# Stages that end with four weight pieces used by token tile, the next stage's first tile turned among them, and rings of seven and five places

## The chip, the cores and the metric

The kernel runs on one core of one Trainium2 chip. The metric is the device time of one execution in microseconds (us); the median of three runs was 2169.57 us (2169.47 to 2170.34).

## The reference, cut to what matters

Two blocks of two layers each work on 256 tokens of 1024 features, in float32. A layer of the first block is

```
x = x + 0.5 * rmsnorm(swiglu(rmsnorm(x, g1), gate, up, down), p1)     # hidden width 2816
x = x +       rmsnorm(token_mixing(rmsnorm(x, g2)) @ w_out, p2)       # chunk band, differential, stick-breaking heads
x = x + 0.5 * rmsnorm(swiglu(rmsnorm(x, g3), gate, up, down), p3)
```

and a layer of the second block is

```
merged = sum over 3 branches of sigmoid gate * (branch output @ w_branch)   # sparse, gated linear, memory attention
x = x + merged @ w_out
x = x + relu(rms_norm(x, g) @ w_up)**2 @ w_down                             # hidden width 4096
```

What matters here: ten stages follow one another (three for each layer of the first block, two for each of the second). Each begins with features of x (a root mean square norm whose scale is applied when the first products are taken out of PSUM) and ends with an output product that is added to x, in the first block after a norm of its own, in the second block plainly.

## The kernel before, in words

**Pieces.** All weights come as one stream of 616 pieces of 128 x 1024 floats, in the order in which TensorE uses them. A float32 product is made of three TensorE products: each piece is split into a rounded high part `hi` and the rest `lo`, as are the activations, and `product` (L513) issues high by high, high by low, low by high. A piece is twelve such products of 512 columns: six for each of the two token tiles (128 tokens each).

**The way of a piece.** SP's program (`piece`, L409) issues its DMA into `raw`; ACT (`round_piece`, L1131) writes the rounded `hi`; POOL (`pool_program`, L484) writes `lo = raw - hi`; TensorE uses it and counts it in the semaphore `used`. Each of the three rings has RING = 4 places (L30). The DMA of piece c waits for `lo` of piece c - 4, the rounding for the landing and for `used` of piece c - 4, POOL for `hi`. ACT's program places the rounding of a piece AHEAD = 3 pieces (L31) ahead of its use, between its other work. `in_mixer` (L476) says which pieces POOL subtracts in four parts of 256 columns; the others are one instruction.

**A stage's start.** `enter_stage` (L598) calls `enter` (L574): TensorE turns token tile 0 of x (`turned_tile`, L559: eight 128 x 128 transposes into four PSUM banks, a pair to a bank), ACT copies each out as `h_hi`, DVE makes `h_lo`. Then TensorE uses the first four pieces for tile 0, turning tile 1 after the second and third, and then the same four pieces for tile 1. Only then are these four counted as used. ACT's `features` (L1162) takes the squares of x for the norm between.

**A stage's end.** `last_rows` (L547) uses the last pieces of the output product (two in the first block, in the second mixer's last branch and its output product; four in the second block's feed-forward) for tile 0, signals `f`, and then for tile 1. ACT (`last_rows`, L1198) takes the squares of the output of tile 0 at `f` (`row_squares`, L1184), the guess of the root (`row_guess`, L1191), then those of tile 1; DVE multiplies by the gain (`row_gain`, L1618) and adds to x in two halves (`row_add`, L1626), each of which counts in the semaphore `x` that the turn waits for. In the second block DVE only adds (`add_plain`, L1644).

**Orders.** Each engine runs its program in order. The mixers' orders are written out by `mix1_order` (L62) and `mix2_order` (L135): attention units stand between strips (four pieces of an input product) and rows (one piece of an output product). Parameter loads stand in SP's program, one after every three pieces.

## Time and profile before

| | |
|---|---|
| profiled execution | 2170.57 us, span 2169.0 us |
| median of the runs | 2169.57 us |
| TensorE busy | 2079.8 us, 96% |
| ScalarE (ACT), VectorE (DVE), GpSimd (POOL) busy | 1057.3, 779.6, 1622.1 us |
| chain that ended last, TensorE's share | 84% |
| mean granted clock of TensorE | 0.987 |

A matmul of 512 columns is shown as 0.39 us long but the next is issued 0.23 us after it: they are pipelined, and a busy TensorE is not one at its peak. The timeline gives start, length, and in brackets the idle time before an instruction and what ended it.

### The profile page before, as it was taken

The numbers are of one execution on the slowest core, as the hardware profiler recorded it, in microseconds if no ns is written. First come the engines' busy times: TensorE is split into PE (matmuls) and PEld (weight loads), VectorE is DVE, ScalarE is ACT, GpSimd is POOL, SyncE is SP. The second block draws the span as 40 slices with busy tenths as digits, with TensorE's granted clock in tenths as the row PEclk, the third lists the DMA queues.
The fourth block names the chain that finished last, engine by engine and source line by source line (L and its number), as shares of the span: only waits on it lengthen the run. The fifth ranks groups of instructions, "written<-read, shape, count | busy, mean of one in ns | idle before, by whom it ended". The sixth has DMA issues, their size and how long they took to land.

```text
span 2169.0 us, 26535 instructions
## 1 busy us (share of the span) xinstructions
PE 2079.8 (96%) x9638; PEld 1648.4 (76%) x9638; DVE 779.6 (36%) x1671; ACT 1057.3 (49%) x1779; POOL 1622.1 (75%) x1412
## 2 busy tenths in 40 slices
PE   7999989999999999899999999999999999999999
PEld 5887666888788766688876777778887677777887
DVE  2524453100201445410045676441015566642111
ACT  5445454544644544554474433654446443455443
POOL 6888654888788865588877576688888756578886
PEclk9999998999999999999999999999999999999999
DMA  6655322555565533256554333345756333334553
GB/s 227 217 184 175 117 99 95 175 193 185 189 226 185 175 118 106 97 198 242 192 212 151 105 108 117 107 146 201 242 179 233 120 104 115 110 115 159 192 183 137
DMA packets 98061, 348.63 MB, mean 161 GB/s; under 512 B 13420, under 2 KB 13964, under 8 KB 97676
## 3 DMA queue, kind: packets, MB, share of 16 engines
q1 hardware_dynamic: 96176, 344.26, 46.0%
q10 hardware_dynamic: 1756, 2.68, 0.3%
q8 instruction: 78, 1.28, 0.2%
q14 instruction: 51, 0.42, 0.1%
HBM read 345.85 MB, written 1.05 MB: 160 GB/s over the span
## 4 chain that ended last, share of the span: by engine, by line
PE 84%; DVE 6%; POOL 5%; ACT 3%; issue 2%; DMA 0%; ACTq 0%; SPq 0%; DVEq 0%
PE psum L514 24%; PE psum L516 23%; PE psum L515 23%; POOL lo L493 5%; PE psum L620 2%; PE psum L851 1%; PE psum L1010 1%; PE psum L658 1%; PE psum L665 1%; PE psum L649 1%; PE psum L675 1%; PE psum L674 1%; DVE psum L1624 1%; PE psum L571 1%; PE psum L667 1%
## 5 line engine op out<-in xcount | busy, mean ns | idle before, releaser
L493 POOL TENSOR_TENSOR lo<-raw,hi 128x256 fp32r<-128x256 f32 (+1 forms) x1408 | 1621.9, 1184 | 535.5 <-ACT hi L1140 534.4
L1140 ACT ACTIVATE hi<-raw 128x1024 fp32r<-128x1024 f32 x616 | 651.4, 1059 | 564.9 <-PE psum L516 539.1
L514 PE MATMUL psum<-hi,h_hi 128*128 128x512 f32 x1632 | 660.9, 405 | 19.3 <-DVE h_lo L1602 11.6
L516 PE MATMUL psum<-hi,h_lo 128*128 128x512 f32 x1632 | 642.7, 394 | 0.0
L515 PE MATMUL psum<-lo,h_hi 128*128 128x512 f32 x1632 | 642.5, 394 | 0.0
L514 PEld LDWEIGHTS psum<-hi,h_hi 128*128 128x128 f32 x1632 | 310.4, 190 | 100.3 <-POOL lo L493 23.8
L516 PEld LDWEIGHTS psum<-hi,h_lo 128*128 128x128 f32 x1632 | 310.0, 190 | 67.4
L515 PEld LDWEIGHTS psum<-lo,h_hi 128*128 128x128 f32 x1632 | 310.8, 190 | 59.9
L514 PE MATMUL psum<-hi,y_hi 128*128 128x512 f32 x832 | 335.3, 403 | 10.4 <-DVE big L2120 4.9
L1664 DVE SCALAR_TENSOR_TENSOR big<-psum,small,big 128x256 f32<-128x256 f32 (+1 forms) x120 | 61.2, 551 | 772.6 <-ACT big L1232 772.6
L516 PE MATMUL psum<-hi,y_lo 128*128 128x512 f32 x832 | 326.5, 392 | 0.0
L515 PE MATMUL psum<-lo,y_hi 128*128 128x512 f32 x832 | 325.8, 392 | 0.0
L514 PEld LDWEIGHTS psum<-hi,y_hi 128*128 128x128 f32 x832 | 157.5, 189 | 48.2 <-DVE big L2120 5.7
L516 PEld LDWEIGHTS psum<-hi,y_lo 128*128 128x128 f32 x832 | 157.1, 189 | 34.3
L515 PEld LDWEIGHTS psum<-lo,y_hi 128*128 128x128 f32 x832 | 157.8, 190 | 30.4
L1275 ACT ACTIVATE soft<-soft,small 128x256 f32<-128x256 f32 (+1 forms) x136 | 61.7, 454 | 218.5 <-DVE small L1700 191.8
L1232 ACT ACTIVATE big<-psum,small 128x256 f32<-128x256 f32 (+1 forms) x120 | 57.2, 528 | 86.8 <-PE psum L516 86.8
L1672 DVE TENSOR_TENSOR y_lo<-psum,y_hi 128x512 fp32r<-128x512 f32 (+1 forms) x60 | 49.5, 824 | 38.3 <-ACT y_hi L1241 38.3
L1602 DVE SCALAR_TENSOR_TENSOR h_lo<-psum,special,h_hi 128x128 fp32r<-128x128 f32 x160 | 44.1, 344 | 47.2 <-ACT h_hi L1157 47.0
L1157 ACT ACTIVATE h_hi<-psum,special 128x128 fp32r<-128x128 f32 x160 | 44.5, 375 | 25.0 <-PE psum L571 25.0
L658 PE MATMUL psum<-consts,soft 128*128 128x128 f32 x188 | 35.8, 295 | 14.2 <-DVE soft L1710 9.5
L1241 ACT ACTIVATE y_hi<-psum 128x512 fp32r<-128x512 f32 (+1 forms) x60 | 42.8, 713 | 13.1 <-PE psum L620 13.1
(265 smaller groups left out, 1608.0 us busy)
## 6 DMA issues: line engine op xcount, KB each, us to landing
raw<-in_stream SPq DMA_DIRECT2D x616, 512.0 KB, 3.3
big<-in_w SPq DMA_DIRECT2D x14, 512.0 KB, 5.2
big<-in_post SPq DMA_DIRECT2D x6, 512.0 KB, 4.9
special<-in_b_merge SPq DMA_DIRECT2D x2, 1536.0 KB, 7.5
memkv<-in_mem SPq DMA_DIRECT2D x2, 1024.0 KB, 6.6
big<-in_band SPq DMA_DIRECT2D x2, 768.0 KB, 4.9
x<-in_x ACTq DMA_DIRECT2D x2, 512.0 KB, 6.1
special<-in_special SPq DMA_DIRECT2D x2, 512.0 KB, 4.9
```

Of the source, the lines that this page charges most:

```text
L493: t = pool.tensor_tensor(M.lo[:, slot, w], M.raw[:, slot, w], f32(M.hi[:, slot, w]), ALU.subtract)
L514: pe.matmul(out, lhs_hi, rhs_hi, start=start, stop=False)
L515: pe.matmul(out, lhs_hi, rhs_lo, start=False, stop=False)
L516: return pe.matmul(out, lhs_lo, rhs_hi, start=False, stop=stop)
L658: t = pe.transpose(psum[:, TURNED, i * P:i * P + P], soft[:, slot, 0, col:col + P], V.ident)
L1140: act.activation(M.hi[:, slot, :], M.raw[:, slot, :], ACT.Copy).then_inc(sem["hi"], 1)
L1157: t = act.activation(out_hi[:, k, toks], psum[:, bank, i * P:i * P + P], ACT.Copy, scale=1.0 if gain is None else gain[:, k:k + 1])
L1232: t = act.activation(act_s[:, m, :], psum[:, bank + m, 0:width], ACT.Silu if gated else ACT.Relu, scale=V.scale[:, m:m + 1])
L1275: t = act.activation(prob[:, w], prob[:, w], ACT.Exp, scale=-1.0, bias=mn[:, i:i + 1], accum_out=total[:, i:i + 1])
L1602: t = dve.scalar_tensor_tensor(out_lo[:, k, toks], psum[:, bank, i * P:i * P + P], gain[:, k:k + 1], f32(out_hi[:, k, toks]), ALU.mult, AL ...
L1664: t = dve.scalar_tensor_tensor(prod_s[:, m, :], psum[:, bank + m, col:col + width], V.scale[:, m:m + 1], act_s[:, m, :], ALU.mult, ALU.mult)
L1672: dve.tensor_tensor(flat(y_lo[:, kt, :]), flat(psum[:, bank:bank + kts // 2, :]), f32(flat(y_hi[:, kt, :])), ALU.subtract).then_inc(sem["y ...
```

## The change

The last four pieces of the output products with a norm, and of the second mixer's, are used by token tile. The next stage's first tile is turned ahead of the last half piece. In the first mixer the halves of the last four pieces stand between the last attention units. `raw` and `lo` share one buffer of seven places, in which POOL overwrites its input; `hi` has five. SP waits for `used` instead of `lo`. Rounding runs four pieces ahead. POOL subtracts whole pieces around the stages' ends and starts. At the start two pieces, not three, are rounded ahead of the first features, and the others behind the first tile's. The diff, without the renamed places:

```diff
-RING = 4
-AHEAD = 3
...
+RING = 7
+RING_HI = 5
+AHEAD = 4
...
         ("unit", k, t) in order for k in ("stick", "band") for t in (3, 5, 7))
-    for i, kt in enumerate(OUT_ORDER[:-2]):
+    for i, kt in enumerate(OUT_ORDER[:-4]):
...
         between()
-    between(len(work))
-    order.append(("last_rows",))
+
+    for m, i in ((0, 0), (0, 1), (1, 0), (0, 2), (1, 1), (0, 3), (1, 2)):
+        while m == 0 and ready() < made[OUT_ORDER[-4:][i]]:
+            between()
+        order.append(("half", m, i))
+        between()
+    order += [("turn",), ("half", 1, 3)]
+    assert not work
...
+
+    with nc.sbuf_tensor("raw", [P, RING, PIECE], F32) as raw:
+        pass
+    lo = sb("lo", [P, RING, PIECE], F32R)
     return Memory(
-        nc=nc, T=T,
-        raw=sb("raw", [P, RING, PIECE]),
-        hi=sb("hi", [P, RING, PIECE], F32R),
-        lo=sb("lo", [P, RING, PIECE], F32R),
+        nc=nc, T=T, raw=raw, lo=lo,
+        hi=sb("hi", [P, RING_HI, PIECE], F32R),
...
         if c >= RING:
-            sp.wait_ge(sem["lo"], c - RING + 1)
+            sp.wait_ge(sem["used"], c - RING + 1)
...
     if c < L * PIECES1:
-        return FFN_PIECES - 4 <= at < PIECES1 - FFN_PIECES + 4 or at >= PIECES1 - 4
-    return at < PIECES2 - 8 * MLP_STRIPS + 4 or at >= PIECES2 - 4
+        return FFN_PIECES + 6 <= at < PIECES1 - FFN_PIECES - 4
+    return 8 <= at < PIECES2 - 8 * MLP_STRIPS - 4
...
             w = slice(i * PIECE // parts, (i + 1) * PIECE // parts)
-            t = pool.tensor_tensor(M.lo[:, slot, w], M.raw[:, slot, w], f32(M.hi[:, slot, w]), ALU.subtract)
+            t = pool.tensor_tensor(M.lo[:, slot, w], M.raw[:, slot, w], f32(M.hi[:, slot_hi, w]), ALU.subtract)
...
-    def last_rows(c, kt, n_kt, a_hi, a_lo, bank):
+    def half_rows(c, m, kt, a_hi, a_lo, bank, stop):
+
+        if m == 0:
+            pe.wait_ge(sem["lo"], c + 1)
+        t = rows_tile(c, m, kt, a_hi, a_lo, bank, False, stop)
+        if m:
+            t.then_inc(sem["used"], 1)
+        elif stop:
+            t.then_inc(sem["f"], 1)
+
+    def last_rows(c, kts, a_hi, a_lo, bank, turn, ylo={}):
         for m in range(MT):
-            for i in range(n_kt):
-                if m == 0:
-                    pe.wait_ge(sem["lo"], c + i + 1)
-                t = rows_tile(c + i, m, kt + i, a_hi, a_lo, bank, False, i == n_kt - 1)
-                if m:
-                    t.then_inc(sem["used"], 1)
-            if m == 0:
-                t.then_inc(sem["f"], 1)
+            for i, kt in enumerate(kts):
+                if m and i == len(kts) - 1 and turn:
+                    turn()
+                if m == 0 and i in ylo:
+                    pe.wait_ge(sem["ylo"], ylo[i])
+                half_rows(c + i, m, kt, a_hi, a_lo, bank, i == len(kts) - 1)
...
         f = n["feats"]
-        turned_tile(src, 0, range(4), banks, ready, until)
...
                     t.then_inc(sem["used"], 1)
-                elif j in (1, 2):
-                    turned_tile(src, 1, range(2 * j - 2, 2 * j), banks, ready, until)
+                elif j > 1:
+                    turned_tile(src, 1, range(2 * j - 4, 2 * j - 2), banks, ready, until)
...
+
+    def turn_x(banks):
+
+        stage = n["stage"]
+        turned_tile(M.x, 0, range(4), banks, "x" if stage else "x_in", 4 * (stage - 1))
...
-    def feed_forward(c, strips, gated, n0):
+    def feed_forward(c, strips, gated, n0, turn_next):
...
         turn(n0 + strips - 1)
-        down(c, n0 + strips - 2)
-        pe.wait_ge(sem["ylo"], n0 + strips)
-        last_rows(c + kts, (strips - 1) % 2 * kts, kts, y_hi, y_lo, 4)
-        return c + 2 * kts
+        if not gated:
+            down(c, n0 + strips - 2)
+            c += kts
+        pe.wait_ge(sem["ylo"], n0 + strips - gated)
+        order = [(strips - s) % 2 * kts + i for s in ((2, 1) if gated else (1,)) for i in range(kts)]
+        last_rows(c, order, y_hi, y_lo, 4, turn_next, {kts: n0 + strips} if gated else {})
+        return c + 4
...
                 rows(c0 + 24 + i, kt, y_hi, y_lo, 0, i == 0)
-            elif what == "last_rows":
-                pe.wait_ge(sem["y1lo"], 7 * layer + Y1_EVENT[OUT_ORDER[-1]])
-                last_rows(c0 + 24 + KD - 2, OUT_ORDER[-2], 2, y_hi, y_lo, 0)
+            elif what == "half":
+                m, i = step[1:]
+                kt = OUT_ORDER[-4:][i]
+                pe.wait_ge(sem["y1lo"], 7 * layer + Y1_EVENT[kt])
+                half_rows(c0 + 24 + KD - 4 + i, m, kt, y_hi, y_lo, 0, i == 3)
+            elif what == "turn":
+                turn_next()
...
-    def mix2(layer, c0):
+    def mix2(layer, c0, turn_next):
...
                 pe.wait_ge(sem["y2lo"], 10 * layer + Y2_EVENT[kt + 1])
-                last_rows(last_c, kt, 2, y_hi, y_lo, ROWS2[1])
+                last_rows(last_c, (kt, kt + 1), y_hi, y_lo, ROWS2[1], None)
...
                 c = last_c + 2
+                turned_tile(V.merged, 0, range(4), (0, 1, 2, 3), "merged", 4 * layer)
...
                 pe.wait_ge(sem["xlo"], 8 * n["feats"])
-                for i in range(4, KD - 2):
-                    rows(c + i, i, h_hi, h_lo, 4, False)
-                last_rows(c + KD - 2, KD - 2, 2, h_hi, h_lo, 4)
+                last_rows(c + 4, range(4, KD), h_hi, h_lo, 4, turn_next)
...
     pe.wait_ge(sem["const"], 16)
+    low, high = (2, 3, 4, 5), (4, 5, 6, 7)
+    turn_low, turn_high = lambda: turn_x(low), lambda: turn_x(high)
     c = 0
+    turn_low()
...
-        c = feed_forward(c, FFN_STRIPS, True, 2 * layer * FFN_STRIPS)
...
-        c = mix1(layer, c)
...
-        c = feed_forward(c, FFN_STRIPS, True, (2 * layer + 1) * FFN_STRIPS)
...
+        c = feed_forward(c, FFN_STRIPS, True, 2 * layer * FFN_STRIPS, turn_low)
...
+        c = mix1(layer, c, turn_high)
...
+        c = feed_forward(c, FFN_STRIPS, True, (2 * layer + 1) * FFN_STRIPS, turn_low)
...
-        c = mix2(layer, c)
...
-        c = feed_forward(c, MLP_STRIPS, False, 4 * FFN_STRIPS + layer * MLP_STRIPS)
...
+        c = mix2(layer, c, turn_low)
...
+        c = feed_forward(c, MLP_STRIPS, False, 4 * FFN_STRIPS + layer * MLP_STRIPS, turn_low if layer < L - 1 else None)
...
         act.wait_ge(landed[slot], 16 * (c // RING + 1))
-        if c >= RING:
-            act.wait_ge(sem["used"], c - RING + 1)
-        act.activation(M.hi[:, slot, :], M.raw[:, slot, :], ACT.Copy).then_inc(sem["hi"], 1)
+        if c >= RING_HI:
+            act.wait_ge(sem["used"], c - RING_HI + 1)
+        act.activation(M.hi[:, slot_hi, :], M.raw[:, slot, :], ACT.Copy).then_inc(sem["hi"], 1)
...
                 between()
-            if squares:
-                squares(m)
+        for m in range(MT if squares else 0):
+            squares(m)
...
             row_guess(0)
-        for i in range(1, n_kt):
-            round_piece(c + i + AHEAD)
-        if norm:
-            row_squares(bank, 1, ("used", c + n_kt))
+        for i in range(AHEAD + 1, n_kt + 3):
+            round_piece(c + i)
...
             if norm:
+                row_squares(bank, 1, ("used", c + n_kt))
+            round_piece(c + n_kt + 3)
+            if norm:
                 row_guess(1)
-            round_piece(c + n_kt + AHEAD)
+            round_piece(c + n_kt + 4)
...
         turn(c, n0 + strips - 1)
-        for i in range(kts):
-            round_piece(c + i + AHEAD)
...
             exp_and_ln()
-        return c + 2 * kts, last_rows(c + kts, kts, 4, gated)
+        else:
+            for i in range(kts):
+                round_piece(c + i + AHEAD)
+            c += kts
+        return c + 4, last_rows(c, 4, 4, gated)
...
                 round_piece(c0 + 24 + step[1] + AHEAD)
-            elif what == "last_rows":
-                rest = last_rows(c0 + 24 + KD - 2, 2, 0, True)
+            elif what == "half" and step[1:] == (0, 0):
+                round_piece(c0 + 24 + KD - 4 + AHEAD)
+            elif what == "half" and step[1:] == (0, 3):
+                rest = last_rows(c0 + 24 + KD - 4, 4, 0, True)
...
     load(V.pre2, T["pre2"].rearrange("l p i k -> p l i k"), "pre")
-    for c in range(AHEAD):
+    exp_and_ln()
+    for c in range(2):
         round_piece(c)
-    exp_and_ln()
     act.wait_ge(sem["pre"], 32)
-    c, rest = 0, lambda: round_piece(AHEAD)
+
+    def rest():
+        for c in range(2, AHEAD + 1):
+            round_piece(c)
+
+    c = 0
...
         row_add(bank, 0)
-        row_gain(gain, bank, 1)
-        return lambda: row_add(bank, 1)
+
+        def second_tile():
+            row_gain(gain, bank, 1)
+            row_add(bank, 1)
+
+        return second_tile
```

## Rows read from the trace of the kernel before

**Rows 1.** Waits of TensorE: engine, line, releaser: us in total, times, longest.
```profile
PE psum L514 <- DVE h_lo L1602: 11.6, 10, 1.6
...
PE psum L514 <- POOL lo L493: 8.7, 9, 1.6
PE psum L571 <- DVE x L1634: 6.9, 6, 1.2
```

**Rows 2.** Timeline of TensorE, a feed-forward's end: start, us, instruction, [idle before <-releaser].
```profile
201.65 0.39 PE L516 MATMUL psum<-hi,y_lo 128*128 128x512 f32 x1
...
204.37 0.39 PE L516 MATMUL psum<-hi,y_lo 128*128 128x512 f32 x1
205.91 1.31 PE L571 MATMUL psum<-consts,x 128*128 128x128 f32 x8 [1.16 <-DVE x L1634]
208.51 0.47 PE L514 MATMUL psum<-hi,h_hi 128*128 128x512 f32 x1 [1.28 <-DVE h_lo L1602]
```

**Rows 3.** Timeline of ACT and of DVE over the same end.
```profile
202.07 1.03 ACT L1187 ACTIVATE big<-psum 128x1024 f32<-128x1024 f32 x1 [1.60 <-PE psum L516]
...
203.29 1.22 DVE L1624 TENSOR_TENSOR psum<-psum,big 128x1024 f32<-128x1024 f32 x1
...
205.10 1.41 DVE L1634 SCALAR_TENSOR_TENSOR x<-psum,small,x 128x512 f32<-128x512 f32 x2
```

**Rows 4.** The page's groups: count | busy us, mean ns | idle before, releaser.
```profile
L1140 ACT ACTIVATE hi<-raw 128x1024 fp32r<-128x1024 f32 x616 | 651.4, 1059 | 564.9 <-PE psum L516 539.1
...
L1672 DVE TENSOR_TENSOR y_lo<-psum,y_hi 128x512 fp32r<-128x512 f32 (+1 forms) x60 | 49.5, 824 | 38.3 <-ACT y_hi L1241 38.3
...
L1241 ACT ACTIVATE y_hi<-psum 128x512 fp32r<-128x512 f32 (+1 forms) x60 | 42.8, 713 | 13.1 <-PE psum L620 13.1
```

**Rows 5.** Timeline of TensorE, the first mixer's end in layer 0.
```profile
356.69 0.66 PE L658 MATMUL psum<-consts,soft 128*128 128x128 f32 x3 [1.59 <-DVE soft L1710]
...
360.47 0.80 PE L514 MATMUL psum<-hi,y_hi 128*128 128x512 f32 x1 [0.93 <-DVE y_lo L1691]
...
368.92 1.32 PE L571 MATMUL psum<-consts,x 128*128 128x128 f32 x8 [1.13 <-DVE x L1634]
371.51 0.77 PE L514 MATMUL psum<-hi,h_hi 128*128 128x512 f32 x1 [1.28 <-DVE h_lo L1602]
```

**Rows 6.** Windows: us; busy of PE, PEld, DVE, ACT, POOL (count); clock; DMA; GB/s.
```profile
357.00:363.80 6.80, 5.87 (x23) 4.52 (x21) 0.98 (x2) 1.33 (x2) 2.79 (x4) 0.50 0.00 0
```

**Rows 7.** Timeline of TensorE, the second mixer's end in layer 0.
```profile
1424.37 0.66 PE L571 MATMUL psum<-consts,big 128*128 128x128 f32 x4 [0.42 <-DVE big L2130]
...
1428.17 0.50 PE L514 MATMUL psum<-hi,h_hi 128*128 128x512 f32 x1 [1.12 <-POOL lo L493]
...
1449.70 0.47 PE L514 MATMUL psum<-hi,h_hi 128*128 128x512 f32 x1 [0.80 <-DVE h_lo L1602]
```

**Rows 8.** Timeline of TensorE, the second block's feed-forward's end in layer 0.
```profile
1626.16 0.50 PE L514 MATMUL psum<-hi,y_hi 128*128 128x512 f32 x1 [0.70 <-POOL lo L493]
...
1641.64 0.50 PE L514 MATMUL psum<-hi,h_hi 128*128 128x512 f32 x1 [0.67 <-POOL lo L493]
```

**Rows 9.** Groups of POOL with shapes apart: count | busy us, mean ns | idle.
```profile
L493 POOL TENSOR_TENSOR lo<-raw,hi 128x1024 fp32r<-128x1024 f32 x352 | 842.0, 2408 | 169.1 <-ACT hi L1140 168.6
L493 POOL TENSOR_TENSOR lo<-raw,hi 128x256 fp32r<-128x256 f32 x1056 | 780.0, 776 | 366.4 <-ACT hi L1140 365.9
```

**Rows 10.** Timeline of DVE and of POOL at two places.
```profile
560.47 0.21 DVE L1631 TENSOR_SCALAR small<-small 128x1 f32<-128x1 f32 x1
...
560.39 2.36 POOL L493 TENSOR_TENSOR lo<-raw,hi 128x1024 fp32r<-128x1024 f32 x1 [1.75 <-ACT hi L1140]
...
1146.51 11.89 DVE L1574 TENSOR_TENSOR small<-small 128x24 f32<-128x24 f32 x1
```

**Rows 11.** Timeline of TensorE, the first stage's fifth piece.
```profile
30.45 0.50 PE L514 MATMUL psum<-hi,h_hi 128*128 128x512 f32 x1 [1.65 <-POOL lo L493]
```

**Rows 12.** DMA issues: KB each, median us from issue to landing.
```profile
raw<-in_stream SPq DMA_DIRECT2D x616, 512.0 KB, 3.3
```

More of the change, by code:

```diff
@@ L411, in piece @@
         n["piece"] += 1
-        slot = c % RING
+        slot, slot_hi = c % RING, c % RING_HI
         if c >= RING:
-            sp.wait_ge(sem["lo"], c - RING + 1)
+            sp.wait_ge(sem["used"], c - RING + 1)
         sp.dma_start(M.raw[:, slot, :], T["stream"][c]).then_inc(landed[slot], 16)
@@ L487, in pool_program @@
     for c in range(PIECES):
-        slot = c % RING
+        slot, slot_hi = c % RING, c % RING_HI
         pool.wait_ge(sem["hi"], c + 1)
@@ L520, in strip_piece @@
         pe.wait_ge(sem["lo"], c + 1)
-        slot = c % RING
+        slot, slot_hi = c % RING, c % RING_HI
         if feats is not None:
@@ L528, in strip_piece @@
                 t = product(psum[:, bank + m, :], a_hi[:, k, m * P:m * P + P], a_lo[:, k, m * P:m * P + P],
-                            hi[:, slot, w], lo[:, slot, w], k == 0, k == KD - 1)
+                            hi[:, slot_hi, w], lo[:, slot, w], k == 0, k == KD - 1)
         t.then_inc(sem["used"], 1)
     def rows_tile(c, m, kt, a_hi, a_lo, bank, start, stop):
-        slot = c % RING
+        slot, slot_hi = c % RING, c % RING_HI
         for i in range(2):
@@ L537, in rows_tile @@
             t = product(psum[:, bank + 2 * m + i, :], a_hi[:, kt, m * P:m * P + P], a_lo[:, kt, m * P:m * P + P],
-                        hi[:, slot, w], lo[:, slot, w], start, stop)
+                        hi[:, slot_hi, w], lo[:, slot, w], start, stop)
         return t
@@ L584, in enter @@
                     t.then_inc(sem["used"], 1)
-                elif j in (1, 2):
-                    turned_tile(src, 1, range(2 * j - 2, 2 * j), banks, ready, until)
+                elif j > 1:
+                    turned_tile(src, 1, range(2 * j - 4, 2 * j - 2), banks, ready, until)
         n["feats"] += 1
     def strip_tile(c, m, j):
-        slot = c % RING
+        slot, slot_hi = c % RING, c % RING_HI
         for i in range(2):
@@ L594, in strip_tile @@
             t = product(psum[:, m, :], h_hi[:, k, m * P:m * P + P], h_lo[:, k, m * P:m * P + P],
-                        hi[:, slot, w], lo[:, slot, w], k == 0, k == KD - 1)
+                        hi[:, slot_hi, w], lo[:, slot, w], k == 0, k == KD - 1)
         return t
+    def turn_x(banks):
+        stage = n["stage"]
+        turned_tile(M.x, 0, range(4), banks, "x" if stage else "x_in", 4 * (stage - 1))
     def enter_stage(c, banks):
@@ L676, in causal_score, with mix1 @@
         free[slot] = ("mn", nxt("mn", 2))
-    def mix1(layer, c0):
+    def mix1(layer, c0, turn_next):
         turned_qk = {}
@@ L1092, in pe_program @@
     pe.wait_ge(sem["const"], 16)
+    low, high = (2, 3, 4, 5), (4, 5, 6, 7)
+    turn_low, turn_high = lambda: turn_x(low), lambda: turn_x(high)
     c = 0
+    turn_low()
     for layer in range(L):
-        enter_stage(c, (2, 3, 4, 5))
-        c = feed_forward(c, FFN_STRIPS, True, 2 * layer * FFN_STRIPS)
-        enter_stage(c, (2, 3, 4, 5))
-        c = mix1(layer, c)
-        enter_stage(c, (4, 5, 6, 7))
-        c = feed_forward(c, FFN_STRIPS, True, (2 * layer + 1) * FFN_STRIPS)
+        enter_stage(c, low)
+        c = feed_forward(c, FFN_STRIPS, True, 2 * layer * FFN_STRIPS, turn_low)
+        enter_stage(c, low)
+        c = mix1(layer, c, turn_high)
+        enter_stage(c, high)
+        c = feed_forward(c, FFN_STRIPS, True, (2 * layer + 1) * FFN_STRIPS, turn_low)
     for layer in range(L):
-        enter_stage(c, (2, 3, 4, 5))
-        c = mix2(layer, c)
-        enter_stage(c, (2, 3, 4, 5))
-        c = feed_forward(c, MLP_STRIPS, False, 4 * FFN_STRIPS + layer * MLP_STRIPS)
+        enter_stage(c, low)
+        c = mix2(layer, c, turn_low)
+        enter_stage(c, low)
+        c = feed_forward(c, MLP_STRIPS, False, 4 * FFN_STRIPS + layer * MLP_STRIPS, turn_low if layer < L - 1 else None)
     assert c == PIECES
@@ L1135, in round_piece @@
         n["rounded"] = c + 1
-        slot = c % RING
+        slot, slot_hi = c % RING, c % RING_HI
         act.wait_ge(landed[slot], 16 * (c // RING + 1))
-        if c >= RING:
-            act.wait_ge(sem["used"], c - RING + 1)
-        act.activation(M.hi[:, slot, :], M.raw[:, slot, :], ACT.Copy).then_inc(sem["hi"], 1)
+        if c >= RING_HI:
+            act.wait_ge(sem["used"], c - RING_HI + 1)
+        act.activation(M.hi[:, slot_hi, :], M.raw[:, slot, :], ACT.Copy).then_inc(sem["hi"], 1)
     def rsqrt(cells):
@@ L1496, in mix2 @@
                 features(None, M.h_hi, (0, 1, 2, 3), rest)
-                for i in range(KD - 2):
+                for i in range(4):
                     round_piece(c + i + AHEAD)
-                rest = last_rows(c + KD - 2, 2, 0, False)
+                rest = last_rows(c + 4, 4, 0, False)
                 c += KD
```

## The prediction

> **What bounds the kernel now.** I read the page first: TensorE is busy 96% of the span and holds 84% of the chain that ended last, so the time is TensorE's, and a gain has to come from its idle time or its clock. The view of waits, kept to TensorE, says what it waits for outside attention: low parts of the features (11.6 us in 10 waits), the residual x (6.9 us in 6) and weight pieces from POOL (8.7 us in 9) [rows 1]. These are small, and the change touches only them. The timeline says where they lie. At the end of a feed-forward with a norm the last product of token tile 0 starts at 201.65, the last of tile 1 at 204.37, the next stage's eight transposes at 205.91 and its first product at 208.51 [rows 2]. Twelve products take 204.37 - 201.65 = 2.72 us, 0.227 us each; a piece is twelve, half a piece (one token tile) 1.36 us.
>
> Why the turn comes late is read from ACT and DVE: squares of tile 0 start at 202.07, the gain at 203.29, x at 205.10 in two halves, done at 206.51 [rows 3]. Counting from t = 201.65 + 0.23, where tile 0's sum is issued, the first half of x is ready at t + 4.0 and the second at t + 4.6, while TensorE has only 2.72 us of tile 1 left. Then the features of the first tile must come back before the first strip.
>
> **The change, part by part.** Durations are the profiled execution's: 2170.57 us with a span of 2169.0; the median of the runs is 1.0 lower, 2169.57.
>
> *Stage ends with a norm, feed-forward to the next (four of them).* From the last product to the first of the next stage TensorE spends 208.51 - 204.37 - 0.23 = 3.91 us, of which the eight transposes need some 1.15; 2.76 us is idle. After the change tile 1 has three halves (4.08 us) between tile 0's end and the turn. That is t + 4.08 against x at t + 4.0: the first four transposes do not wait, the last four wait some 0.15 us for the second half of x. The last half piece (1.36 us) then stands between the turn and the first strip, and covers the 1.28 us that it waits for h_lo today. What is late next is the second token tile. Its squares start 0.2 us after the last product, and the rounding of the fourth piece (1.06 [rows 4]) now stands between them and the guess, so the first half of x comes not 4.0 but some 4.3 us after the stage's end; TensorE asks for it after three half pieces, at 4.08. That fourth piece, rounded by 2.4, has its low part (2.41 us [rows 9]) at 4.85, and it is wanted at about 4.9. I put 0.25 us on the two together and 0.1 on the turn: 2.76 - 0.35 = 2.4 us gained, times four is 9.6. Tile 0 now runs over only 2.72 us of older pieces before it needs the last strip's y_lo, where it had 5.44: ACT's copy (0.71 in the mean) and DVE's subtraction (0.82) [rows 4] fit under that, so 0.
>
> *The first mixer's end (two).* Today TensorE idles 1.59 us for a probability, 0.93 for y_lo, 1.13 for x and 1.28 for h_lo [rows 5]; counted from issue to issue (0.23 after a product, where the rows count from its end, 0.39) each is 0.16 more, 5.6 us in all. The last four pieces' halves now stand between the band units. The wait for the probability gets one half as cover: 1.75 - 1.36 leaves 0.4. The one for y_lo gets one too and goes. But the last half of tile 0 comes after that unit, and only one half of tile 1 is left before the turn: x is ready 4.0 us after, the cover is 1.36, so 2.65 us of wait stays. With 0.4, 0.15 and 0.25 as above 3.45 stays and 2.1 goes: 4.2 for both.
>
> *The second mixer's end and the branch's output product (two).* TensorE waits 0.42 us for the merged x at 1424.37, 1.12 for POOL at 1428.17 and once more as long some 15 us later, and 0.80 for h_lo at 1449.70 [rows 7]. Five places for high parts let rounding go one piece (2.72 us) further ahead, the merged tile's second half turns one piece later, and the last four pieces are subtracted whole: 2.41 us against 4 x 0.776 = 3.10 as the mean [rows 9]. The waits are 0.42 + 1.12 + 1.12 + 0.80 and 4 x 0.16, 4.1 us; the first two pieces of slack meet all but some 0.4, which I leave standing: 3.7 each, 7.4 for both.
>
> *The second kind of feed-forward.* It ends by token tile over four pieces already. Its waits are 0.70 for POOL at 1626.16, 0.80 for h_lo as at 1449.70, and for POOL 0.67 at 1641.64 and a like one of 0.48 before it [rows 8]; with 4 x 0.16 that is 3.3 us. Its x needs no norm and is long ready at the turn, and with a fifth place the pieces are there. All 3.3 goes, and 0.9 for the same first wait in the last stage.
>
> *The start.* The fifth piece waits 1.65 us for its subtraction [rows 11], for its place is not free; with five places it is rounded before that. Rounding two pieces instead of three ahead of the first features lets these start earlier, but they wait for their gains from DMA. 1.65 + 0.16 and 0.2 more: 2.0.
>
> *Places and queues.* SP now waits for a piece's use seven back, not for the subtraction four back, and its parameter loads stand behind the same wait and shift with it. Six pieces (16.3 us at 2.72) lie between that use and the piece's own turn; landing (3.3 [rows 12]), rounding and subtraction take 3.3 + 1.06 + 2.41 = 6.8. Rounding may start two pieces (5.4 us) after the issue, so it does not wait either. An earlier issue gains nothing and a later one up to 9 us costs nothing: 0. The moved squares put the stage's scale some 1 us later; the first strip ends about as late, so 0 too.
>
> *Subtraction in place.* raw and lo now share their memory. No row shows POOL writing over its own input. Below: 2.41 us as today, there is no reason for less. Above: the mean of the quartered form, 3.10 a piece. I take 2.41, because the whole form is the row that keeps its shape; the upper end is a rival below.
>
> *DVE beside whole subtractions.* Around the ends pieces are subtracted in quarters today and whole after the change. A small step of the norm took 0.21 us at 560.47, inside a whole subtraction from 560.39 to 562.75 [rows 10]: such steps do not wait, 0. The Trainium skill ("SBUF — State Buffer", section "Who interferes with whom") says that a DVE instruction with two SBUF inputs and a GpSimd instruction that reads SBUF exclude one another for the whole instruction. By that rule alone a root's step would wait for one subtraction, 2.4 us; here the trace differs, for such a step took 11.89 us at 1146.51 [rows 10], longer than any one subtraction. The stage's root is such work. Its four steps (by the norm's 0.21 some 0.8 us) follow ACT's guess, and the next piece's rounding (1.06 us) follows the same guess, so they end just before POOL starts. I take 0; what it costs when caught is a rival below.
>
> *Clock.* At 357.0 to 363.8 and 370.7 to 377.4 the granted clock is 0.50, the lower of the two levels (1.2 GHz), right behind the waits of the first mixer's end; TensorE is busy 5.87 us in the first [rows 6] and as long in the second, so half of 11.7, 5.9 us, is lost. The same end in the other layer has no such stretch, so I take half of that as gone: 3.0. Ends: 6 gained, or as much lost if two such stretches appear.
>
> **Sum.** 9.6 + 4.2 + 7.4 + 3.3 + 0.9 + 2.0 + 3.0 = 30.4. 2170.57 - 30.4 = 2140.2 in the profiled execution, 2139 for the median.
>
> **Rivals.**
> - *The turn arrives before x.* Were the norm's chain 1.4 us longer than today (its squares behind a rounding, or x behind DVE's features), each of the six normed ends would give back 1.4 and the second tile as much: 6 x 1.4 to 6 x 2, about 10 us, 2149. For it: the margin at the turn is 0.1 us. Against: ACT's and DVE's orders put nothing new ahead of tile 0's chain.
> - *More slack than counted.* Both slow stretches go (3 more), what I left standing at the ends goes (4 x 0.35, 2 x 0.8 and 2 x 0.4, 3.8 us), and one more such stretch in the attention goes (3): 2140 - 9.8, 2130. For it: whole subtractions and the fifth place help in every stage. Against: TensorE waits only 8.7 us for POOL in all.
> - *The root caught behind POOL.* Three pieces can be subtracted before the strip's eviction needs the root, 3 x 2.41 = 7.2 us. The feed-forwards have a second strip (10.9 us) as cover; the four mixers' entries, whose first attention step wants the first strip one piece later, would show some 6 each: 24, so 2164. For it: 11.89 us in rows 10. Against: the margin above, some 0.3 us, which holds by the order on ACT.
> - *Slower: subtraction in place.* If POOL takes longer over its own input, feed-forward stages turn POOL-bound: TensorE needs 2.8 us for a piece there (2.72 and its share of the strips' transposes), and the feed-forwards hold 392 pieces, all whole. It decides from 2.8 us; at 3.0 it costs 392 x 0.2 = 78 us, 2218; slower than before from 2.88. For it: no row excludes it. Against: the operation, its shape and its bytes are the same.
> - *The change moves the wait only.* If x, not the order, sets the next stage, the 27 us stay where they are: 2167 to 2172. For it: at the first mixer's end half of it does. Against: rows 3 at the other ends.
>
> **How the numbers follow.** Forecast 0.58, with its own range of 2131 to 2147; the turn before x 0.15; more slack 0.15; the root caught 0.04; in place and slower 0.04; the wait only moved 0.04, within 0.2%, which is about what a measurement of this kernel tells from no change. 2124 to 2154 holds the first three but for their tails, 0.85. Faster 0.58 + 0.15 + 0.15 + 0.04 = 0.92, less 0.01 for mishaps not named: 0.91; same 0.04; slower 0.05.
>
> **What would show it.** Right: at the feed-forwards' ends the eight transposes stand before the last half piece with under 0.3 us of wait, and the next strip follows without a gap; at the first mixer's end 2.5 us of wait for x stays; the waits for POOL at the last branch product and at the last piece of the second block's feed-forward are gone; whole subtractions still mean 2.4 us. Wrong: a whole subtraction over 2.8 us; a wait for x over 1 us at the plain ends; a root's step over 2 us at an entry; landings that rounding waits for in a feed-forward.

## The result, and the profile after

The four runs after took 2129.81, 2130.66, 2131.50 and 2141.14 us, median 2131.08; before, on the same chip, 2169.95. The ratio of the two is 0.9831 (95% interval 0.9802 to 0.9861). Timed again beside the experiments, the same kernel took 2131.23 to 2141.49 us, median 2138.59, ratio 0.9855 (0.9834 to 0.9876). The forecast was 2139 us, 2124 to 2154. The spread of ten microseconds between runs of one program is taken up below. The profiled execution is the quickest of the four: 2129.81 us, span 2128.3 us, mean granted clock 0.995 (before 0.987).

The waits of TensorE after the change, in the columns of [rows 1]:

```profile
PE psum L589 <- DVE x L1675: 5.0, 2, 2.5
...
PE psum L524 <- DVE h_lo L1643: 4.7, 1, 4.7
...
PE psum L524 <- POOL lo L503: 3.3, 5, 1.3
```

These answer to 11.6, 6.9 and 8.7 us before. One wait for `h_lo` is left, at the very start; two for x, at the first mixer's ends; five for POOL, one at the start and four in the second mixers. The first of those four, at the last branch's output product of [rows 7]:

```profile
1399.22 0.50 PE L524 MATMUL psum<-hi,h_hi 128*128 128x512 f32 x1 [0.65 <-POOL lo L503]
```

TensorE at the feed-forward's end of [rows 2], timeline:

```profile
206.34 0.39 PE L526 MATMUL psum<-hi,y_lo 128*128 128x512 f32 x1
206.56 1.27 PE L589 MATMUL psum<-consts,x 128*128 128x128 f32 x8
207.59 0.48 PE L524 MATMUL psum<-hi,y_hi 128*128 128x512 f32 x1
...
209.06 0.40 PE L524 MATMUL psum<-hi,h_hi 128*128 128x512 f32 x1
```

No bracket stands in it: the eight transposes follow the third half of tile 1 at once, the last half covers the return of the features, and the first strip follows that. At the first mixer's end the wait for x stayed, and the stretch at half clock of [rows 6] behind it is not there in layer 0 (timeline; then a window with the columns of [rows 6], its clock 1.00):

```profile
362.12 1.31 PE L589 MATMUL psum<-consts,x 128*128 128x128 f32 x8 [2.52 <-DVE x L1675]
```

```profile
361.00:367.00 6.00, 4.88 (x25) 3.98 (x26) 4.80 (x14) 5.15 (x13) 4.71 (x2) 1.00 0.38 135
```

POOL by form, as [rows 9]; a whole subtraction over its own input takes what one into another buffer took (2408 ns):

```profile
L503 POOL TENSOR_TENSOR lo<-raw,hi 128x1024 fp32r<-128x1024 f32 x436 | 1040.7, 2407 | 277.7 <-ACT hi L1171 277.3
L503 POOL TENSOR_TENSOR lo<-raw,hi 128x256 fp32r<-128x256 f32 x720 | 546.1, 794 | 249.7 <-ACT hi L1171 249.4
```

The start is later. Timeline of ACT, then of TensorE; the last line is SP's, with seven pieces issued in a row. The wait of 1.32 us answers to the 1.65 of [rows 11], but there the fifth piece waited; here the fifth follows the fourth without a wait, and it is the sixth that waits:

```profile
16.27 1.91 ACT L1188 ACTIVATE h_hi<-psum,special 128x128 fp32r<-128x128 f32 x7 [7.03 <-DMA special<-in_pre]
...
17.77 0.77 PE L524 MATMUL psum<-hi,h_hi 128*128 128x512 f32 x1 [4.71 <-DVE h_lo L1643]
...
36.48 0.50 PE L524 MATMUL psum<-hi,h_hi 128*128 128x512 f32 x1 [1.32 <-POOL lo L503]
...
0.74 3.37 SPq L425 DMA_DIRECT2D raw<-in_stream  x7
```

**Where the time went.** In each trace I took the end of the last product of chosen pieces, and compared the lengths of the stretches between them, after less before:

| stretch | predicted, us | measured, us |
|---|---|---|
| start, to the sixth piece | -2.0 | +3.3 |
| four ends of normed feed-forwards | 4 x -2.4 = -9.6 | -2.85, -2.51, -2.85, -4.27 |
| first mixer's two ends, their clock with them | -4.2 - 3.0 | -7.0 and -0.7 |
| second mixer (two) | 2 x -3.7 = -7.4 | -6.4 and -5.1 |
| second kind of feed-forward's end | -3.3 | -3.6 |
| last stage | -0.9 | -1.1 |
| first mixer's attention (two) | 0 | -2.8 and -4.9 |
| sum | -30.4 | -40.7 |

Stretches of granted clock 0.50, the lower level, add up to 54.6 us of the span before and 20.5 after. Half of that is lost while TensorE has work: 27.3 and 10.2 us at most, so up to 17 of the 40.7 us are clock, spread over most rows of the table. The last row but one was not in the forecast at all. In it the trace shows a small product of DVE (two sums of an attention unit, one element in each partition). Timelines of DVE and of POOL, before and after:

```profile
230.23 0.17 DVE L1753 RECIPROCAL small<-small 128x2 f32<-128x2 f32 x1 [0.74 <-ACT soft L1275]
230.43 4.03 DVE L1754 SCALAR_TENSOR_TENSOR small<-small 128x1 f32<-128x1 f32 x1
...
228.88 5.57 POOL L493 TENSOR_TENSOR lo<-raw,hi 128x256 fp32r<-128x256 f32 x8
```

```profile
230.69 0.17 DVE L1798 RECIPROCAL small<-small 128x2 f32<-128x2 f32 x1 [0.74 <-ACT soft L1309]
230.89 0.55 DVE L1799 SCALAR_TENSOR_TENSOR small<-small 128x1 f32<-128x1 f32 x1
...
230.69 0.74 POOL L503 TENSOR_TENSOR lo<-raw,hi 128x256 fp32r<-128x256 f32 x1
```

Before, it ends at 234.46, where a run of POOL's quarters ends (228.88 + 5.57 = 234.45); TensorE waits 1.75 us for its unit, and the window from 234.1 to 240.9 that follows runs at clock 0.50. After, it ends at 231.44, with the one quarter that it meets (230.69 + 0.74 = 231.43), though that run goes on.

### The profile page after: what moved, and what is told of

The parts are those of the page before. It is cut to its first block, busy times and chain, and to the rows that moved or that the text cites. A ratio compares the mean times of both kernels' runs of the same rounds, so it can differ in the third digit from the quotient of the medians.

```text
span 2128.3 us, 26283 instructions
## 1 busy us (share of the span) xinstructions
PE 2062.5 (97%) x9638; PEld 1639.6 (77%) x9638; DVE 771.5 (36%) x1671; ACT 1051.5 (49%) x1778; POOL 1586.7 (75%) x1160
## 4 chain that ended last, share of the span: by engine, by line
PE 89%; DVE 4%; ACT 3%; issue 1%; POOL 1%; DMA 1%; ACTq 0%; DVEq 0%
PE psum L524 26%; PE psum L526 25%; PE psum L525 25%; PE psum L642 2%; PE psum L880 1%; PE psum L1039 1%; PE psum L683 1%; PE psum L589 1%; POOL lo L503 1%; PE psum L690 1%; PE psum L674 1%; PE psum L700 1%; PE psum L699 1%; DMA special<-in_pre 1%; PE psum L717 1%
## 5 line engine op out<-in xcount | busy, mean ns | idle before, releaser
L503 POOL TENSOR_TENSOR lo<-raw,hi 128x256 fp32r<-128x256 f32 (+1 forms) x1156 | 1586.5, 1403 | 527.4 <-ACT hi L1171 526.7
L642 PE MATMUL psum<-consts,big 128*128 128x128 f32 x304 | 42.9, 272 | 0.0
```

The source lines that it names most:

```text
L503: t = pool.tensor_tensor(M.lo[:, slot, w], M.raw[:, slot, w], f32(M.hi[:, slot_hi, w]), ALU.subtract)
L642: t = pe.transpose(psum[:, bank + i // 2, (i % 2) * S + m * P:(i % 2) * S + m * P + P], V.work_prod[:, m, i * P:i * P + P], V.ident)
```

## The experiments

All are edits of the kernel after, but for the one with the places alone. Theory at the outset: the order takes away the waits for x and `h_lo`, the places those for POOL, and the start is late because of a queue.

**The start.** Edit: `if c == 4: sp.wait_ge(sem["pre"], 32)` in SP's `piece`.

> The kernel after, but SP waits for the two small gain loads of ACT's queue before it issues the fifth piece; so four pieces stand in the queues at the start, as before the change, not seven. Theory (the gains wait in the DMA engines behind three more pieces of 512 KB): the gains land some 9.9 us after their issue, not 12.6, ACT's wait of 7.03 us for them falls to some 4, the first strip starts some 3.3 to 4.5 us earlier (at 13.3 to 14.5 us, not 17.8), and the whole is 3 to 4.5 us faster than the kernel after, about 2127 us. Rival (the gains are late because ACT asks for them or comes to them in another order): the first strip stays at 17 to 18 us and the time at 2130 to 2131.

Measured: 2135.28 us (2132.70 to 2141.07), ratio to before 0.9856 (0.9834 to 0.9878). The theory was right about the start and not about the whole. DMA issues (KB, median us to landing) of the kernel after and of this one, then TensorE's first strip here:

```profile
special<-in_pre ACTq DMA_DIRECT2D x2, 24.0 KB, 12.6
```

```profile
special<-in_pre ACTq DMA_DIRECT2D x2, 24.0 KB, 9.8
```

```profile
14.09 0.76 PE L526 MATMUL psum<-hi,h_hi 128*128 128x512 f32 x1 [1.02 <-DVE h_lo L1645]
```

The first strip begins 3.7 us earlier, and the sixth piece ends 4.3 us earlier. (The run with the order alone, below, issues four pieces at the start too, and its first strip also begins at 14.09.) The sixth piece's wait for POOL stays, 1.33 us. But up to the middle of the first attention 3.8 us are given back: there TensorE waits 3.70 us for a unit's probabilities, because the small product of DVE took 6.02 us in this profile, and again in the other layer. A run below takes that up.

**The turn's place.** Edit, in `last_rows` and likewise in `mix1_order`:

```
-                if m and i == len(kts) - 1 and turn:
-                    turn()
...
                 half_rows(c + i, m, kt, a_hi, a_lo, bank, i == len(kts) - 1)
+                if m and i == len(kts) - 1 and turn:
+                    turn()
```

> The kernel after, but the next stage's first tile is turned behind the last half piece instead of ahead of it; the four pieces by token tile stay. Theory (the half piece between the turn and the first strip hides the 1.28 us in which the features come back, and the three halves ahead of the turn hide the wait for x): at each of the nine ends some 1.3 us of wait for h_lo comes back between the turn and the first strip; in the first mixer's two ends the wait for x shrinks by the same 1.3 us, so nothing changes there. 7 x 1.3 = 9 us slower than the kernel after, 2140 us, and up to 5 us more if stretches at half clock come back. Rival (the four halves ahead do all the work, the turn's place is worth nothing since ACT and DVE are still late): 2130 to 2133.

Measured: 2149.82 us (2147.00 to 2155.92), ratio to before 0.9921 (0.9902 to 0.9940): slower than the kernel after, by more than expected. The waits of TensorE:

```profile
PE psum L524 <- DVE h_lo L1643: 11.4, 10, 4.7
...
PE psum L589 <- DVE x L1675: 3.6, 7, 1.2
```

The nine ends show 6.7 us of wait for `h_lo` again (11.4 - 4.7), and each normed feed-forward's end is 1.15 us longer, the others about 1.0; at the first mixer's ends the turn's place is worth nothing, as expected. That is 7 x 1.1 = 8 us. The rest of this profile is the held product of DVE (3.0 and 2.6 us), a like one in the second mixer (2.7), and half clock (22.2 us lost at most, 10.2 in the kernel after).

**The places alone.** Edit of the kernel before: `RING = 7`, `RING_HI = 5`, `AHEAD = 4`, `lo` over `raw`, SP waiting for `used`; order and quarters untouched.

> The kernel before, with the places alone: lo written over raw, seven places for these and five for hi, rounding four pieces ahead, SP waiting for a piece's use. Order of work, and which pieces are subtracted in quarters, as before. Theory (the places remove only waits for POOL and ACT's rounding; the waits for x and h_lo at the ends are the order's): the ends of the normed feed-forwards keep their 2.76 us, the start loses some 3 us, the waits for POOL in the second mixer and in the second kind of feed-forward go, 2 x (2.2 + 1.9) + 1.8 = 10 us; about 2163 us, 2158 to 2168. Rival (the deeper places are the change, and the order is only along for the ride): 2140 to 2150.

Measured: 2159.76 us (2156.92 to 2161.85), ratio 0.9960 (0.9947 to 0.9973). The waits of TensorE for POOL outside attention (8.7 us before) are gone from the list; what the order is for is still there:

```profile
PE psum L516 <- DVE h_lo L1604: 14.8, 10, 4.7
...
PE psum L573 <- DVE x L1636: 6.9, 6, 1.2
```

So the places are worth 8 to 9 us and do nothing for the ends in the first block. All of it lies in the second block: in this profile the second mixers are 3.3 and 3.4 us shorter than before, the second kind of feed-forward 3.1, the last stage 1.1, against 1.0 us lost at the start.

**The order alone.** Edit: `RING = RING_HI = 4`, `AHEAD = 3`, `raw` and `lo` apart, SP waiting for `lo`; the last rounding in `last_rows` goes `AHEAD` pieces ahead.

> The kernel after with the places of before: four each for raw, hi and lo apart, rounding three pieces ahead. The order of work stays (four pieces by token tile, the turn among them). Theory (the places are what lets the order pay: four pieces used by tile hold all four places until tile 1 has used the first, so the next stage's pieces come late): at each end a wait for POOL of 1 to 3 us stands in place of the wait for x and h_lo; 2158 to 2168 us, hardly faster than before. Rival (order and places add up: all of the change less the 8 us of the places alone): 2140 to 2150 us.

Measured: 2174.51 us (2172.53 to 2175.94), ratio to before 1.0021 (1.0012 to 1.0031): not even as fast as before. The waits of TensorE:

```profile
PE psum L523 <- POOL lo L502: 38.5, 43, 4.0
...
PE psum L588 <- DVE x L1674: 5.0, 2, 2.5
...
PE psum L523 <- DVE h_lo L1642: 1.8, 4, 1.2
```

The waits for x are down as in the kernel after, those for `h_lo` nearly so, and 38.5 us of waits for POOL stand in their place: four pieces used by token tile keep all four places until tile 1 has used the first. (The rest of ACT's order stays as it was written for the larger rings; what part of the 38.5 us that makes was not separated.) The second mixers are 1.9 and 4.3 us longer than before in this profile, where the places alone made them shorter. Places alone gain 8 to 9 us and order alone loses some 5; together they gain 30 to 39. The theory had the mechanism and set its price too low; the rival, that they add up, falls.

**Whole subtractions at the ends.** Edit: `in_mixer` as before the change.

> The kernel after, but with POOL subtracting the pieces around the stage ends in quarters again, as before the change (4 x 0.78 us in place of 2.41). Theory (a piece is then 0.7 us later, and the ends leave no more than some 0.3 us of margin for the fourth piece): 0.3 to 0.8 us at each of the nine ends and entries, 3 to 7 us slower, 2134 to 2138 us. Rival (the fifth place gives slack enough, and quarters let DVE in between sooner, so they cost nothing or help): 2128 to 2132.

Measured: 2147.35 us (2143.05 to 2150.05), ratio to before 0.9904 (0.9886 to 0.9922). TensorE waits 7.5 us in 12 times for POOL, where it waited 3.3 in 5: 4.2 us, inside the 3 to 7 expected. The profile is 20.2 us longer than that of the kernel after: the rest is the small product, held here too (6.25 and 6.45 us, which costs 3.8 and 3.4 without the clock), and half clock, 18.8 us lost at most against 10.2.

**Is the held product chance?** The kernel after, unchanged.

> The kernel after, unchanged, timed again beside the next three. In its first profile DVE's small product of the first attention unit's two sums (one element in each partition, two inputs from SBUF) took 0.55 us at 230.89, between two of POOL's quarters; in the profiles of the kernel before and of four variants it took 4.0 to 6.4 us, to the end of POOL's run, and TensorE waited 2 to 4 us for it, in each layer. Theory (whether it gets in between two of POOL's instructions is chance, not the change's doing): the times fall into two groups, some at 2128 to 2131 us and some at 2137 to 2141 us, and the median lies anywhere between. Rival (the change's places bring it in between, and the variants lose that): all runs at 2128 to 2132, the product at 0.55 us again.

Measured: 2131.23, 2136.52, 2140.65 and 2141.49 us. The profiled run was 2140.65. Timeline of DVE and of POOL, and TensorE's wait:

```profile
230.06 0.17 DVE L1798 RECIPROCAL small<-small 128x2 f32<-128x2 f32 x1 [0.74 <-ACT soft L1309]
230.27 5.98 DVE L1799 SCALAR_TENSOR_TENSOR small<-small 128x1 f32<-128x1 f32 x1
...
220.05 16.18 POOL L503 TENSOR_TENSOR lo<-raw,hi 128x1024 fp32r<-128x1024 f32 x21 [4.54 <-ACT hi L1171]
...
236.69 0.48 PE L683 MATMUL psum<-consts,soft 128*128 128x128 f32 x1 [3.70 <-DVE soft L1803]
```

The product ends at 236.25, POOL's run at 220.05 + 16.18 = 236.23. The two profiles of one and the same program differ at the two first attentions, by 4.7 and 6.9 us (6.5 of the 11.6 without half clock); their spans are 10.9 us apart, and elsewhere they agree within some 0.6 us a stretch. The rival falls: one and the same program shows both outcomes, so the change by itself does not bring this gain. Among the eight profiles with this instruction and no pause, the kernel before and five others hold the product and two let it in, each time alike in both layers. Of the kernel before there is one profile; whether it too is let in at times, no run shows.

**One input less.** Edit: `dve.tensor_scalar(c_ratio, total, inverse, minus_lam, mult, mult)` in place of `scalar_tensor_tensor`.

> The kernel after, but DVE's small product takes its two factors as per-partition scalars, so that one tensor input is left in place of two; POOL's run is not interrupted. Theory (an instruction with two SBUF tensor inputs is held, one with a single one is not, as the reciprocal ahead of it, 0.17 us beside POOL): the product takes 0.2 us in every run; the next instruction with two inputs, the sum of the two probabilities, is held in its place for up to 5 us, so the time is 2130 to 2141 us as chance has it. Rival (the small product alone is the trouble): 2128 to 2131 us in all runs.

Measured: 2141.47 us (2134.47 to 2146.93), ratio to before 0.9872 (0.9851 to 0.9893). Timeline of DVE:

```profile
230.35 0.28 DVE L1799 TENSOR_SCALAR small<-small 128x1 f32<-128x1 f32 x1
...
230.66 5.82 DVE L1803 SCALAR_TENSOR_TENSOR soft<-soft,small 128x128 f32<-128x128 f32 x1
```

With one tensor input the same product is not held (0.28 us, in all sixteen), and the next instruction with two is held in its place (in layer 0; in layer 1 it got through). So at this place it is the form of the instruction, as expected, and to change one of two gains nothing. The same section of the Trainium skill that the prediction weighed ("SBUF — State Buffer", "Who interferes with whom") says that a DVE instruction with at most one SBUF input, outside the two-port performance modes, does not contend with GpSimd; the 0.28 us agrees. One tensor input alone is not enough, though. In the kernel after's second profile a copy of 24 elements in each partition was held for 15.50 us, which took 1.35 in the first:

```profile
58.07 15.50 DVE L2264 COPY extra<-extra 128x24 f32<-128x24 f32 x1
```

No trace shows in which mode an instruction ran.

**A pause for POOL.** Edit in `pool_program`, after the wait for `hi`:

```
+        if c < L * PIECES1 and c % PIECES1 == FFN_PIECES + 8:
+            pool.wait_ge(sem["prob"], 20 * (c // PIECES1) + 1)
```

> The kernel after, but POOL waits ahead of the ninth piece of each first mixer (74 and 238 of the stream, wanted by TensorE some 8 us later) for the first unit's probabilities; so its run of subtractions has an end where DVE's small product comes. Theory (the product is held by the run, not by one instruction): it takes under 2.5 us in every run, the wait of 4 us on TensorE is gone, the first mixer's middle is as in the kernel after at its best, and all runs lie at 2128 to 2132 us with less spread. Rival (the wait for the product hides nothing, or POOL's pause makes a piece late): 2135 us or more, with a wait of TensorE for POOL in the first mixer.

Measured: 2132.13 us (2127.68 to 2135.76), ratio to before 0.9825 (0.9807 to 0.9842). The product took 0.22 us in both layers, and both first attentions are within 0.1 us of the kernel after at its best. By its time alone the run cannot be told from the kernel after. The spread is still 8 us: in the profile (2135.76) another instruction with two inputs, the addition of a gated branch in the second mixer, was held, where it took 1.37 us in the kernel after:

```profile
1382.94 10.42 DVE L2174 TENSOR_TENSOR big<-big 128x1024 f32<-128x1024 f32 x1
```

**Start and pause together.**

> POOL's pause of the run above and SP's wait for the small gain loads ahead of the fifth piece together. Theory (the start's 4.3 us and the held product are independent): the start gains its 4.3 us again and nothing is given back in the first mixer; 2124 to 2127 us, faster than the kernel after at its best. Rival (what the start gains is given back later whatever POOL does): 2129 to 2136 us.

Measured: 2127.25 us (2126.29 to 2132.01), ratio to before 0.9813 (0.9795 to 0.9830). The start's 4.3 us are kept through the first attention this time; the rival falls.

**The second pause.** Edit, with the two above:

```
+        layer, at = divmod(c - L * PIECES1, PIECES2)
+        if layer >= 0 and at in (72, 73):
+            pool.wait_ge(sem["branch"], 4 * layer + at - 69)
```

> The start's wait and POOL's pause in the first mixer as before, and a second pause: POOL waits ahead of the pieces 72 and 73 of each second mixer's block until DVE has added the gated branch to the merged sum of the first and of the second token tile. In two profiles of earlier variants that addition (two SBUF inputs of 1024 elements) took 10.4 us, to the end of POOL's run, in others 1.4 us. Theory (the same chance, at another place): it takes under 2.5 us; the runs with 2132 us and the like go, the median is 2124 to 2127 us with less spread. Rival (the pause makes the four pieces of the output product late, which stand behind it): a wait of TensorE for POOL of 1 to 3 us at the second mixer's output product, 2128 to 2132 us.

Measured: 2126.86 to 2128.30 us in five runs, median 2127.71, ratio to before 0.9805 (0.9792 to 0.9819). The addition took 1.60 and 1.50 us, TensorE's waits for POOL are 2.8 us in 5 times, and the spread of these five runs is 1.4 us, not ten. That is in part luck: the run below has the same two pauses, and its four runs spread over 6.1 us, at mean clocks from 0.992 to 0.996. The median did not fall below that of the run above, nor to the 2124 to 2127 us expected. This version beats both kernels: its interval lies below that of the kernel after timed again (0.9834 to 0.9876), though not clear of the first measurement's (0.9802 to 0.9861), and its slowest run (2128.30) is below the quickest of the kernel after's eight (2129.81).

**More cover for x at the first mixer's end.** Edit of the run above: `(0, 3), (1, 1)` in place of `(1, 1), (0, 3)`.

> The kernel of the run above, with the second half of tile 1 moved behind the last half of tile 0 at the first mixer's end; so two halves (2.72 us) in place of one stand between tile 0's end and the turn. Theory (x is ready 4.0 us after tile 0's end, whatever stands between; the half moved is taken from the cover of y_lo): the wait for x at the turn falls from 2.52 to some 1.2 us, and a wait for y_lo of up to 1.3 us appears ahead of the last half of tile 0; the sum is the same within 0.5 us. Rival (y_lo is ready without that cover): 1.3 us gained in each of the two layers, and fewer stretches at half clock behind them; 2.6 to 6 us faster than the run above.

Measured: 2126.38 us (2122.86 to 2128.95), ratio to before 0.9799 (0.9783 to 0.9815), not to be told from the run above. Waits of TensorE at the first mixer's end in layer 0:

```profile
352.45 0.50 PE L531 MATMUL psum<-hi,y_hi 128*128 128x512 f32 x1 [0.93 <-DVE y_lo L1744]
...
357.98 1.31 PE L596 MATMUL psum<-consts,x 128*128 128x128 f32 x8 [1.16 <-DVE x L1683]
```

2.52 became 0.93 + 1.16 = 2.09: the half only moves the wait, as the theory has it. 0.4 us of wait is saved in each layer, of which the stage's end shows 0.2 to 0.4.

## Why the prediction was right, and where it was not

**Normed feed-forward ends: right.** 2.5 to 2.85 us each without clock, where 2.4 was forecast. The narrow margin held: the transposes start 0.22 us after the third half's last product, as one product follows another. The 0.35 us that I left standing was not there. The run with the turn last splits it: about 1.1 us is the turn's place, the rest the two more halves ahead of it (the run with the places alone leaves these ends as they were).

**First mixer's ends: right.** 2.65 us of wait for x were to stay; 2.52 did. The run with the other order shows that it is a sum of two covers and no place for a gain. The clock there: in layer 0 both stretches of [rows 6] are gone, in layer 1 a new one stands at 890; forecast -7.2 with the clock, measured -7.7. That the sum agrees rests on the clock: 7.0 us came in one layer and 0.7 in the other.

**Second mixer, second feed-forward, last stage: right in size, and by the places.** -11.4 in the second mixers against -7.4, up to 5 of it half clock that I had not counted; -3.6 and -1.1 against -3.3 and -0.9. The run with the places alone, in the old order and with the old quarters, has nearly all of it but the half clock (-3.3 and -3.4, -3.1, -1.1), so the places are what pays there; the run with the order alone makes the second mixers longer. Not all the waits went: the sign "the waits for POOL at the last branch product ... are gone" came half true, with 0.65 us left of 1.12 in layer 0 and 0.81 of 1.09 in layer 1.

**The step that failed: the start.** The prediction put: "Rounding two pieces instead of three ahead of the first features lets these start earlier, but they wait for their gains from DMA", and "An earlier issue gains nothing and a later one up to 9 us costs nothing". The earlier issue costs: three more pieces of 512 KB in the queues brought the gains to 12.6 us where 9.9 was, and 2.0 gained became 3.3 lost. The wait for POOL that was to go only moved, from the fifth piece (1.65 us) to the sixth (1.32). With SP's wait for the gains the start is 1.0 us ahead of the kernel before, not 2.0, and there the sixth piece still waits 1.33 us. I had looked at what the pieces wait for, not at what waits behind them.

**The terms that were mis-sized: clock and chance.** The clock's term was 3.0, for the first mixer's ends, where it held; the whole profile has up to 17. And 7.7 us came from the first attention, up to 5.1 of it half clock, where the forecast said nothing. The rows held a hint: the 11.89 us in [rows 10] were read as a danger for the root at an entry, while the same hold was being paid for in both first attentions before the change. In the profile in which it struck again (2140.65 us) the time is the 2140.2 of the sum. That agreement is partly luck too: the start's 5.3 us too little stands against clock too much.

**A sign of being wrong that showed.** "A root's step over 2 us at an entry" was one. Timelines of DVE at the entry of layer 0's second mixer, before, then after, with POOL after:

```profile
1138.02 0.20 DVE L1583 TENSOR_SCALAR small<-small 128x2 f32<-128x2 f32 x1
```

```profile
1113.39 3.87 DVE L1624 TENSOR_SCALAR small<-small 128x2 f32<-128x2 f32 x1
...
1109.56 7.68 POOL L503 TENSOR_TENSOR lo<-raw,hi 128x256 fp32r<-128x256 f32 x11
```

This step, with one tensor input, was held to the end of POOL's run (1109.56 + 7.68 = 1117.24; the step ends at 1117.26). The forecast's argument counted the four steps behind ACT's guess; this one stands ahead of the guess and was left out. It cost TensorE nothing: from 1100 to 1130 the only idle time that its timeline shows is 0.47 us, and the same 0.47 stood there before. So the term of 0 held by slack and not by its reason.

**The rivals.** "The root caught behind POOL" named the mechanism and the wrong place: its hold at an entry came, but the price was paid in the first attention. "The turn arrives before x" is out by the waits of x, "in place slower" by 2407 ns, "the wait only moved" by the ends. "More slack than counted" (2130) is the time of the quick runs, and by other causes: the slow stretches did go in layer 0, but the held product made the rest.

## What to carry to other kernels

An order of work and the buffers behind it are one change: pieces that are used twice, once for each tile, hold their places longer, and without more places the order loses what it gains. Here the places alone gave the second block's part; the first block's ends needed both. When a ring is deepened, look at what its first fill is queued ahead of; small loads on which the first stage depends come before the deep fill. When runs of one program differ by more than the edit is worth, compare two profiles of the same program first, and give the engine that runs without a pause a wait at the place where another needs memory.

## What the hardware showed that was not expected

- A DVE instruction with two SBUF tensor inputs that met a run of POOL subtractions was, by chance, let in at the next end of one (0.55 us) or held to the end of the whole run (4.0 to 6.5 us, 10.4 us in the second mixer). Some instructions with one tensor input were held as well (3.87 and 15.50 us). The Trainium skill ("SBUF — State Buffer", section "Who interferes with whom") has the two exclude one another for an instruction; here the wait went over some eight quarters of 0.71 us. What decides between the two stays open: the same program showed both, with the same 0.2 us between the quarter's start and the product's.
- When DVE was let in, POOL paid: one quarter beside the 1.37 us addition was 1.7 us long, not 0.74.
- A 24 KB load took 9.8 us with four pieces of 512 KB issued at the same time on another queue, and 12.6 us with seven.
- Stretches at the lower clock level come and go between runs of one program: runs of the kernel after had mean clocks from 0.991 (the two slowest, 2141.14 and 2141.49 us) to 0.995 (the quickest, 2129.81).
